# A transformer trunk step: output-stage loads asked for inside the recurrence, tiles by completion, routing from x1, second picks gathered beside the first

## The reference

```
sh1, sc1, ga1, sh2, sc2, ga2 = silu(cond) @ w_ada + b_ada      # one set for context, one for latent tokens
h    = rmsnorm(x, norm1_g) * (1 + sc1) + sh1
proj = h @ w_in
y_rw = (headnorm(rwkv scan forward + backward) * ln_w + ln_b + bonus) * (sigmoid(lg) @ rw_g2)
y_gl = rmsnorm(GLA forward + backward) * silu(og)
x1   = x + ga1 * (concat(y_rw, y_gl) @ w_out)
h2   = rmsnorm(x1, norm2_g) * (1 + sc2) + sh2
logits = h2 @ [w_group, w_expert] + biases                      # 4 groups, 16 experts
pick the best group, its two best of 4 experts, weights from the softmaxes
x2   = x1 + ga2 * sum over picks of weight * (silu(h2 @ w3[e]) * (h2 @ w1[e])) @ w2[e]
y    = rmsnorm(x2, final_g)
```

## Time and profile before

| | us |
|---|---|
| three runs, lowest / median / highest | 1055.82 / 1058.53 / 1061.81 |
| the profiled execution, its own time | 1057.45 |
| its span in the profile | 1055.7 |
| busy in the span: TensorE / its weight loads | 899.8 / 555.5 |
| busy: VectorE / ScalarE / GpSimd | 570.0 / 321.6 / 148.5 |
| mean granted TensorE clock (1 is full speed) | 0.921 |

### The profile page before, as it was taken

One profiled execution on the slowest core, in us unless ns is written; L12 is line 12 of the kernel. 1 busy time (PEld: TensorE's weight loads), 2 busy tenths in 40 slices (PEclk: granted clock), 3 DMA queues, 4 the chain that ended last, 5 costly groups with the idle time before them and its releaser, 6 DMA issues.

```text
span 1055.7 us, 21668 instructions
## 1 busy us (share of the span) xinstructions
PE 899.8 (85%) x8995; PEld 555.5 (53%) x8995; DVE 570.0 (54%) x954; ACT 321.6 (30%) x564; POOL 148.5 (14%) x295
## 2 busy tenths in 40 slices
PE   2799999988994999248888888869995889999995
PEld 0445445545552655147777777734454644444442
DVE  1432046697997188735566565345634335445455
ACT  2320110230000435445665664312111122222213
POOL 5000111111002000053224331000000110010041
PEclk9899999997996899569999999989887799999998
DMA  9800422232231220011221120181115669999958
GB/s 336 331 1 24 149 81 90 81 128 95 78 114 46 80 90 0 13 26 31 53 38 29 32 51 17 36 279 60 61 40 170 208 221 367 370 367 367 345 117 217
DMA packets 119007, 138.22 MB, mean 131 GB/s; under 512 B 49916, under 2 KB 85112, under 8 KB 118904
## 3 DMA queue, kind: packets, MB, share of 16 engines
q1 hardware_dynamic: 110072, 112.32, 32.7%
q0 software_dynamic: 3744, 13.63, 4.8%
q10 hardware_dynamic: 5088, 10.82, 2.7%
HBM read 118.79 MB, written 17.97 MB: 130 GB/s over the span
## 4 chain that ended last, share of the span: by engine, by line
PE 69%; DVE 14%; issue 6%; DMA 4%; ACT 3%; POOL 2%; SPq 1%; ACTq 0%; DVEq 0%; POOLq 0%
PE bank L1813 63%; PE bank L1817 6%; DVE rk_r L1321 3%; ACT region L876 2%; DMA region<-in_w_ada_dram 1%; DMA region<-in_w_out_dram 1%; DMA region<-expert_rows_dram,pick_slots 1%; POOL region L867 1%; DVE region L1321 1%; ACT ada_row_buffers L876 1%; DVE cl_b L1223 1%; DVE region L1802 1%; POOL yg_b L784 1%; DVE vtok_b L1432 1%; DVE cl_b L1733 0%
## 5 line engine op out<-in xcount | busy, mean ns | idle before, releaser
L1813 PE MATMUL bank<-region 64*64 64x64 f32 (+2 forms) x4064 | 483.9, 316 | 50.1 <-issue 28.6
L1813 PEld LDWEIGHTS bank<-region 64*64 64x64 f32 (+1 forms) x4064 | 269.5, 154 | 251.8 <-issue 237.4
L876 ACT ACTIVATE region<-bank 128x256 f32<-128x256 f32 (+3 forms) x232 | 107.5, 463 | 435.1 <-PE bank L1813 286.2
L1817 PE MATMUL bank<-ident,region 128*128 128x128 f32 (+2 forms) x423 | 73.5, 309 | 33.9 <-DMA scratch<-in_gla_gk_dram 12.6
L1817 PEld LDWEIGHTS bank<-ident,region 128*128 128x128 f32 (+2 forms) x423 | 53.6, 157 | 54.1 <-issue 31.1
L1813 PE MATMUL bank<-region,rk_r 128*128 128x512 f32 x160 | 72.0, 603 | 0.0
L1321 DVE SCALAR_TENSOR_TENSOR rk_r<-region,vec,rk_r 128x512 f32<-128x512 f32 x64 | 54.2, 847 | 2.3
L1784 DVE TENSOR_SCALAR region<-region 128x256 f32<-128x256 f32 x16 | 4.7, 294 | 93.6 <-ACT region L876 93.6
L853 POOL DMA_INDIRECT rk_r<-h_rows_dram,slot_tokens x16 | 15.5, 969 | 264.2 <-DVE slot_tokens L1748 135.8
L1549 DVE TENSOR_TENSOR region<-bank,region 128x256 f32<-128x256 f32 x60 | 25.5, 425 | 49.9 <-PE bank L1813 48.5
L1813 PEld LDWEIGHTS bank<-region,rk_r 128*128 128x128 f32 x160 | 30.3, 194 | 34.5 <-issue 34.5
(11 more groups left out here) (264 smaller groups left out, 1122.7 us busy)
## 6 DMA issues: line engine op xcount, KB each, us to landing
region<-in_moe_w_dram SPq DMA_DIRECT2D x36, 1024.0 KB, 10.5
region<-in_w_ada_dram SPq DMA_DIRECT2D x12, 2048.0 KB, 9.0
region<-in_w_in_dram SPq DMA_DIRECT2D x6, 2048.0 KB, 7.8
cl_b<-in_moe_w_dram SPq DMA_DIRECT2D x12, 1024.0 KB, 12.2
expert_rows_dram<-yg_b ACTq DMA_DIRECT2D x14, 512.0 KB, 6.8
region<-in_w_out_dram SPq DMA_DIRECT2D x2, 2048.0 KB, 12.4
a_rows_dram<-region SPq DMA_DIRECT2D x20, 128.0 KB, 2.7
region<-inverse_rows_dram SPq DMA_DIRECT2D x20, 128.0 KB, 3.1
```

The source lines that it names most:

```text
L876: return act.activation(out, in_, func, **kw)
L1813: return pe.matmul(out, lhsT, rhs, start=start, stop=stop)
L1817: return pe.transpose(out, in_, ident[0:n, 0:n])
```

## The change

What it does:

- The tiles of the output stage go by completion, `ORD` = 0, 3, 2, 4, 1. Indices n count places in this order, t = `ORD[n]` is the tile.
- The loads of the output stage are requested inside the recurrence. The head-norm vectors and gate weights, then W_out, wait for the last `r_and_k`; W_out goes into `cl_b` and `rk_r` (`wo`), which are free then. The routing weights and all of x (straight into `x1`) wait for the X64 product of step 8; the up weights of expert 0 for the Y rows of step 8. `final_g` is requested after the h2 stores.
- Parts of the output stage move into the last steps: statistics and head norm of place 0, statistics of place 1, gate and `turn_y` of place 0, six of the twelve row vectors. The other six stand behind the first output product.
- Routing takes x1 itself: the router weights are multiplied by the gain (1 + sc2) * norm2_g for each condition (`wr_gain`), the shift sh2 @ w plus bias is a row of its own (`routing_shift`, `wr_shift`, job rc), and VectorE scales the router's bank by the row's reciprocal root. `turn_h2` becomes `turn_x1`; h2 is still made and stored, for the gathers.
- The output product is multiplied into `xt` and added to x1.
- At the end the first pick's rows are added in memory by the gather with accumulate, as before; the second pick's rows are gathered plainly into buffers of their own (`second_rows`) and added by VectorE. The two gathers of a tile are issued one behind the other.
- Two gain buffers (`gain_b`), begun by ScalarE before it stores the expert before. TensorE's `count_known` moves behind the selections.

The diff, cut to its core:

```diff
+        ORD = [0, 3, 2, 4, 1]
...
-            sp.wait_ge(s_rwdone, 1)
+            sp.wait_ge(s_rk, NS)
             sp.dma_start(lnw, rw_ln_w[0].partition_broadcast(P)).then_inc(s_wo, 16)
...
             for h in range(2):
-                sp.dma_start(ring[:, h], w_out_v[:, :, h * 512:(h + 1) * 512]).then_inc(s_wout, 16)
-            sp.dma_start(xt, x_prompt[0]).then_inc(s_xt, 16)
+                sp.dma_start(wo[h], w_out_v[:, :, h * 512:(h + 1) * 512]).then_inc(s_wout, 16)
+            wait_filled(sp, "X64", NS - 2, 1)
...
+            sp.dma_start(x1[:, 0], x_prompt[0]).then_inc(s_xt, 16)
+            sp.dma_start(x1[:, 1:NT], x_sample[0].rearrange("(t p) n -> p t n", p=P)).then_inc(s_xt, 16)
...
+            wait_filled(sp, "Y", NS - 2, 1)
             load_up(0)
-            for t in range(NT):
-                if t < NT - 1:
-                    sp.wait_ge(s_x1, t + 1)
-                    sp.dma_start(xt, x_sample[0, t * P:(t + 1) * P, :]).then_inc(s_xt, 16)
-                sp.wait_ge(s_h2, t + 1)
+            for n in range(NT):
+                t = ORD[n]
+                sp.wait_ge(s_h2, n + 1)
                 sp.dma_start(h2_dram[t * P:(t + 1) * P, :], h2).then_inc(s_h2d, 16)
...
-                    if i in (1, 2):
+                    if i == 1:
+                        sp.wait_ge(s_h2, NT)
+                    elif i == 2:
                         wait_filled(sp, "out", NT - 1, 1)
...
-                for j in range(2):
-                    for t in range(NT):
-                        if j == 1:
-                            pool.wait_ge(s_yg[t], 32 * r + 16)
-                        pool.indirect_dma_start(out=x1[:, t], ... compute_op=ALU.add).then_inc(s_yg[t], 16)
+                wait_filled(pool, "ug", LE - 1 if r == 0 else i)
+                for t in range(NT):
+                    if t == NT - 1:
+                        wait_filled(pool, "ug", i)
+                    pool.indirect_dma_start(out=x1[:, t], ... compute_op=ALU.add).then_inc(s_yg[t], 16)
+                    pool.indirect_dma_start(out=second_rows[t], ...).then_inc(s_yg[t], 16)
...
# VectorE, recurrence loop
+                if s == NS - 1:
+                    head_norm(0)
                 if new:
                     grown("X32", s)
...
+                if H == NS - 3:
+                    wait_result(dve, "Y", 0, 1)
+                    head_stats(0)
+                if s == NS - 1:
+                    gated(0)
+                    wait_result(dve, "Y", NS - 5, 1)
+                    head_stats(1)
# VectorE, output stage
+            head_norm(1)
+            gated(1)
+            routing_rows()
+            head_stats(2)
+            head_norm(2)
+            for n in range(NT):
+                residual(n)
+                if n + 2 < NT:
+                    gated(n + 2)
+                if n + 3 < NT:
+                    head_stats(n + 3)
+                if n < NT - 1:
+                    h2_rows(n)
+                if n + 3 < NT:
+                    head_norm(n + 3)
+                if n >= 2:
+                    router_logits(n - 2)
+            router_logits(NT - 2)
+            h2_rows(NT - 1)
             router_logits(NT - 1)
...
                 def rows_complete(t):
                     dve.wait_ge(s_yg[t], 32 * (r + 1))
+                    own(TT(x1[:, t], x1[:, t], second_rows[t], ALU.add))
# ScalarE, last place
+                if n == NT - 1:
+                    x1_columns(n)
+                x1_rstd(n)
# TensorE, recurrence loop
                 if back:
                     wu_rows(H)
+                if H == NS - 1:
+                    turn_y(0)
+                    row_vector("ga1", 1, 0)
...
                     chunk_maps(H)
+                if H == NS - 1:
+                    row_vector("ga1", 1, 1)
+                    routing_shift()
...
                     state_from_state(H, 0)
+                    if H == NS - 1:
+                        row_vector("sc2", 0, 0)
+                        row_vector("sc2", 0, 1)
...
+                if s == NS - 1:
+                    pe.wait_ge(s_g2, 1)
+                    gate(0)
+                    row_vector("ga1", 0, 0)
+                    row_vector("ga1", 0, 1)
+            def routing_shift():
+                pe.wait_ge(s_wr, 64)
+                b = open_bank("rc")
+                for c in range(2):
+                    for k in range(KT):
+                        ins = mm(b[:, c * NR:(c + 1) * NR], modv[:, 3 * KT + k, c:c + 1].broadcast_to([P, P]), wr[:, k, :], start=k == 0, stop=k == KT - 1)
+                finish(ins)
# TensorE, output stage
+            for n in range(NT):
+                if n + 1 < NT:
+                    gate(n + 1)
...
+                if n + 1 < NT:
+                    turn_y(n + 1)
+                if n == 0:
+                    for key in late_rows:
+                        row_vector(*key[1:])
+                if n >= 1:
+                    turn_x1(n - 1)
+                if n >= 2:
+                    router(n - 2)
+            router(NT - 2)
+            turn_x1(NT - 1)
             router(NT - 1)
```

More of the change, by code:

```diff
@@ L1578, in added_rows, with head_stats @@
                     out_of(TT(y3[:, hp::2], bank(("Y", h, hp))[:, 0:RC * HD].rearrange("p (h i) -> p h i", h=RC), y3[:, hp::2], ALU.add), "Y", h, hp)
+            mu8 = small[:, 104:112]
+            s3 = sqj.rearrange("p (h i) -> p h i", h=NH)
+            def head_stats(n):
+                t = ORD[n]
+                y3 = yacc[:, t].rearrange("p (h i) -> p h i", h=NH)
+                own(dve.tensor_reduce(out=mu8, in_=y3, axis=AXX, op=ALU.add))
+                own(TS(mu8, mu8, 1.0 / HD, None, ALU.mult))
+                own(TT(y3, y3, bc(mu8, 2, HD), ALU.subtract))
+                own(TT(s3, y3, y3, ALU.mult))
+                tell(dve.tensor_reduce(out=rs8, in_=s3, axis=AXX, op=ALU.add), s_y)
@@ new lines, in gated, with routing_rows @@
+            def gated(n):
+                wait_filled(dve, "gate", n)
+                if n >= 1:
+                    wait_filled(dve, "yT", n - 1, 0)
+                out_of(TT(ya, yacc[:, ORD[n]], bank(("gate", n))[:, :], ALU.mult), "gate", n)
+            def routing_rows():
+                dve.wait_ge(s_wr, 64)
+                for c in range(2):
+                    ins = TT(wr_gain[:, c], wr, bc(gscv[:, 1, :, c], 2, NR), ALU.mult)
+                    own(ins) if c == 0 else tell(ins, s_wrg)
+                wait_filled(dve, "rc")
+                out_of(TT(wr_shift, bank(("rc",))[:, 0:2 * NR].rearrange("p (c n) -> p c n", c=2), bc(br, 1, 2), ALU.add), "rc")
@@ new lines, in residual @@
+            def residual(n):
+                t = ORD[n]
+                cnd = 0 if t == 0 else 1
+                for h in range(2):
+                    wait_filled(dve, "out", n, h)
+                    if n == 0 and h == 0:
+                        wait_result(dve, "rowb", "ga1", 1, 1)
+                    out_of(TT(xt[:, h * 512:(h + 1) * 512], bank(("out", n, h))[:, :], grow_b[0][cnd][:, h * 512:(h + 1) * 512], ALU.mult), "out", n, h)
+                dve.wait_ge(s_xt, 32)
+                tell(TT(x1[:, t], x1[:, t], xt, ALU.add), s_x1)
@@ new lines, in h2_rows, with router_logits @@
+            def h2_rows(n):
+                t = ORD[n]
+                cnd = 0 if t == 0 else 1
+                dve.wait_ge(s_x1r, n + 1)
+                if n == 0:
+                    wait_result(dve, "rowb", "sh2", 1, 1)
+                else:
+                    dve.wait_ge(s_h2d, 16 * n)
+                own(STT(h2, x1[:, t], rstd[:, n:n + 1], grow_b[1][cnd], ALU.mult, ALU.mult))
+                tell(TT(h2, h2, grow_b[2][cnd], ALU.add), s_h2)
+            def router_logits(n):
+                t = ORD[n]
+                cnd = 0 if t == 0 else 1
+                wait_filled(dve, "router", n)
+                dve.wait_ge(s_x1r, n + 1)
+                out_of(STT(lgt[:, t], bank(("router", n))[:, 0:NR], rstd[:, n:n + 1], wr_shift[:, cnd], ALU.mult, ALU.add), "router", n)
@@ L1770, in rows_of @@
                     at = r * (LE // 2) + e // 2
+                    gain = gain_b[e % 2]
                     dve.wait_ge(s_gain, i + 1)
[L1772 removed]
+                    own(STT(gain, ga2b[:, 0], slot_w[:, NE + e:NE + e + 1], gain, ALU.mult, ALU.add))
                     if at:
```

342 lines of the change are left out of this document (164 added, 178 removed).

## The result

The changed kernel takes 1044.57 us (median of 4 runs, 1041.86 to 1047.16) against 1057.17 for the kernel before on the same chip: ratio 0.99, interval 0.9868 to 0.9931. It is faster by 1.0 to 1.2%; the forecast was 2.1%.

A forecast was written before the change was run, and what follows sets the result against it. TensorE was taken to bound both the output stage and the experts. Last logits 19.9 us earlier plus 1.8 us at the end make 21.7, giving 1035.8 from the profiled execution, 1036.8 from the median: 1036 us, range 1029 to 1046.

The forecast's parts named there:

- Loads: Last recurrence steps: W_out lands about 666, before its use at 688; x, routing and expert 0 weights cost nothing.
- I add its work at the full level: TensorE from 667.30 on as one full-clock queue: 115.4 us of work, last tile's x1 transposed by 782.7.
- The shift: Routing shift, 16 matmuls before the first output tile: 3.7 us, bounds 0 (in holes) and 7.1 (half level).
- Late mask: Tile 0's head statistics on VectorE delay the last masks: 2.1 of 3.1 us reach TensorE, bounds 0 and 3.1.
- The output stage: First output tile at about 688, tiles 18 to 19 us apart after the second, last logits at 791.2.
- the 2 us for them: Clock loss charged for two boundaries between output tiles that hold a router: 2 us, bounds 0 and 6.
- The rule on transposes: Transposes don't count as busy for the clock like matmuls; every two-set boundary would fall, some 5 us more.
- The tail at the half level: Two routers and transposes after the last large matmul, 9 us, at half clock: 1 us charged, bounds 0 and 5.
- Logits to experts: Last logits to first expert product: unchanged at 26.1 us; nothing charged for expert weights beside the gather, bound 2 us.
- The end: Final gathers in pairs, selections sooner, five more VectorE additions: last final row 1.8 us earlier, from 4 earlier to 3 later.
- The rivals: the first: Half the clock gain missing: falls at all four tile boundaries, whole tail at half level; 1043 to 1045, chance 0.22.
- the end gave more, not less: Judges the rival that the end gives nothing back: +3 in place of -1.8, 1040 to 1041, chance 0.10.

The follow-up runs named there:

- e1: The changed kernel run again without edits: 1044.09 us, ratio 0.99 to the kernel before.
- e3: Changed kernel with W_out, x and expert 0's first up weights all requested after the recurrence's end: 1053.00 us, ratio 0.9969 to the kernel before.
- e2: Changed kernel with x and expert 0's first up weights requested after the recurrence's end, W_out left early: 1037.72 us, ratio 0.982 to the kernel before.
- e4: Changed kernel with 14 of the routing shift's 16 matmuls left out, so its logits are not the reference's: 1040.34 us, ratio 0.9845.
- e5: Changed kernel with tile 0's head statistics split: means behind the last mask, squares behind X16, ScalarE's part moved too: 1042.17 us, ratio 0.9871.
- e6: Changed kernel with expert 2's up weights requested only once expert 0's gathered tokens have landed: 1041.22 us, ratio 0.9861.
- e8: Changed kernel with the end's gathers in the old order, first picks then second ones, both added in memory: 1047.82 us, ratio 0.9934.
- e9: Changed kernel with x and expert 0's weights late, W_out in 8 paced pieces, routing weights requested between the third and fourth: 1036.41 us, ratio 0.9838.
- e15: Changed kernel with x and expert 0 late, routing shift behind the first tile, expert 2's weights behind the gather, W_out paced; statistics unsplit: 1034.74 us, ratio 0.9807.
- e12: Changed kernel with x and expert 0 late, statistics split, shift behind first tile, expert 2's weights behind the gather, W_out in 8 paced pieces: 1032.68 us, ratio 0.9802.
- e16: The same kernel as e12, run again with more rounds: 1034.03 us, ratio 0.9788 to the kernel before.
- e18: e12 with the routing weights requested behind the eighth piece of W_out: 1032.56 us, ratio 0.978 to the kernel before.
- e7: Changed kernel with all 16 routing-shift matmuls issued behind tile 0's turn, ahead of the late row vectors: 1041.64 us, ratio 0.9869.
- e14: Changed kernel with only the x rows requested after the recurrence's end, expert 0's weights left early: 1037.55 us, ratio 0.9826.

## Why the prediction was right in direction and too large in size

Between the profiled executions the gain is 15.6 us where the sum had 21.7; between medians it is 12.6 and, in e1, 11.0. The 3 to 4 us between these two ways of counting are mostly the spread of single executions: e1's profiled execution has the same parts and ends 2.5 us later, and 2.2 of these lie ahead of the starting place of the table, which alone moves by 4.9 between the executions. Step by step, by the profiles:

- **Loads: the failed step.** "Their cost is nothing" was right for SP and for W_out's landing (about 664, forecast 666) and wrong for TensorE: with the loads beside it, it stalls with ready inputs and loses its clock. I had named the queues that the requests pass and not the one that, by the timing of its packets, feeds TensorE. Price by e3: 5.9 us, of which x and expert 0 are 5.1 (e2). The step still pays: without the early request the wait is 13.85.
- **TensorE, "I add its work at the full level": the second.** The shift was sized right (3.65, forecast 3.7). Its clock was not: bound 7.1 was for the shift itself, but the half level came behind it, on the vectors and state products of 688 to 695, 3.8 us by e4. It falls there without a stall near it (e2) and with none over 0.3 us at all (e3), so this is a second term and not a part of the first.
- **Late mask**: 2.4 us of idle time, forecast 2.1. Right in size; e5 shows that taking it away gives nothing as long as the instructions come when they do.
- With 11.3 us late at the first output product (699.3, forecast 688), these are 5.9, 3.8 and 0.3; 1.3 is open, as much as identical executions differ there. Counted from the table's starting place, which this execution reached 0.6 earlier than the one before, 1.9 is open.
- **The output stage** was 6.1 us better than the sum, 97.1 us from first product to last logits against 103.2. All four boundaries stay at 1.00, so the 2 us for them were not needed. About 3 more is work priced too high: I had added busy times, and the pitch from one group of records to the next is shorter (a tile 13.74 in place of 13.9, 699.27 to 713.01). The tail gave the last 1.2: 5.3 us from the last transpose to the last logits, forecast 6.5. The rule on transposes that spoke against the change ("TensorE: Matmul & The Clock Gate", "Part 4: PE-mode transpose", in the Trainium skill) would have cost 5 that did not come. Two sets of transposes (1.75) and a router between large products cost no clock here, in this or in any other profile of the changed kernel and its variants; the old boundary that fell had 1.40 us of idle time besides, and whether that made the difference was not tried by itself. Transposes took 0.87 a set (forecast 0.93). The tail at the half level came as forecast (0.50 in 792 to 797).
- **Logits to experts**: 28.2 against 26.1; my bound of 2 was the truth, and e6 gives 1.9 us back.
- **Experts**: unchanged, as forecast. 179.1 and 179.2.
- **The end**: 2.9 earlier in the profile, forecast 1.8; the gather order by itself gives 3.5 (e8). The landings were mis-sized: 8.6 in place of 10.6 in the median. The early selections by themselves show no gain: e8 has them with the old gathers, and its last part, 34.2, is no shorter than the 33.7 before. From 1019.76 on VectorE's 4.0 us per tile sets the pace, which the sum had.

11.3 - 6.1 + 2.1 - 1.1 = 6.2, and 21.7 - 6.2 is the profiled 15.5. The forecast's range held the measured time by luck: 9.7 us of losses that it did not have and 6.1 of output stage that it had priced too high met in one sum. The rivals: the first had about the right price (1043 to 1045) for the wrong reason, since the boundaries kept their clock; the end gave more, not less. None named the stalls.

## What to carry over

Moving a load into "idle" DMA time is free only if nothing else lives on these engines: beside many short matmuls a burst can show as "issue" with ready inputs, here 5.5 us of it. Request early what is needed first (W_out early saves a wait of some 14 us and costs 0.8 by e2 against e3, which is within the spread) and let what is needed later wait: x and expert 0's weights late bring the ratio from 0.99 to 0.982 (e2). W_out in paced pieces besides took most of the stalls away (e9, e15), but no gain in time is shown for that alone. The later place of the light products and of expert 2's weights goes with ratios of 0.978 to 0.981 in e12, e15, e16 and e18. Light products behind a large one cost less clock than in front of it, 1.6 us against 3.8, and not nothing: one profile in which the clock stayed up (e7) was not the rule. And when an engine's late input is removed, look what it meets next before counting the gain.

## What the runs showed of the hardware beyond the forecast

- TensorE stalls of 1.2 to 4.2 us with ready inputs, all 23 ending 2.3 to 3.5 us after the start of the 1-us window that holds an instruction packet; stalls in 640 to 700 sum to 5.5 us with bursts at a DMA share of 1.0, 0.5 with the same bytes of W_out paced and the rest later, 0.3 with no large load. With idle DMA engines there are some too (1.72 us in e14, 1.08 in the kernel before).
- The clock fell from 1.00 to 0.50 (1.2 GHz) behind 3.65 us of 20-column products that followed row vectors and 64-row products, with or without stalls ahead (the changed kernel, e3). With the same products behind 14 us of 512-column ones it stayed at 1.00 (2.4 GHz) in one profile (e7) and fell to 0.50 for a shorter time, 1.6 us lost, in five others.
- Two sets of transposes and a 20-column router between output products, without idle time, left the clock at 1.00 in every profile.
- Gathers with expert weights beside them: first expert product 32.5 us behind the last router at a DMA share of 1.08, 30.6 at 0.57.
